# Gate and up matmuls of a feed-forward stage on 256 tokens at a time

## The reference, cut to what matters

```python
D_MODEL = 1024; SEQ = 512; D_FF = 2816
...
x = x + mix @ w_out[l]
h2 = rms_norm(x, g_ffn[l])
x = x + (jax.nn.silu(h2 @ w_ffn_gate[l]) * (h2 @ w_ffn_up[l])) @ w_ffn_down[l]
```

## Time and profile before

| | |
|---|---|
| median of 2 timed runs | 974.32 us (973.59 to 975.04) |
| span of the profiled execution, first to last instruction | 970.9 us |
| TensorE busy in the span | 915.0 us, 94%, 4492 matmuls |
| weight loads busy | 756.9 us, 78%, 4492 loads |
| VectorE, ScalarE busy | 398.1 us (41%), 361.3 us (37%) |
| stage of L1399 | 602.0 to 842.1 us of the span |

### The profile page before, as it was taken

How to read it: one execution, slowest core, us unless ns; L and a number is a source line. 1 busy time by engine, 2 the same in 40 slices (tenths; PEclk the granted TensorE clock), 3 DMA queues, 4 the chain that set the end, 5 groups by cost and what they waited for, 6 DMA issues and landing times.

```text
span 970.9 us, 13078 instructions
## 1 busy us (share of the span) xinstructions
PE 915.0 (94%) x4492; PEld 756.9 (78%) x4492; DVE 398.1 (41%) x554; ACT 361.3 (37%) x532; POOL 189.3 (19%) x256
## 2 busy tenths in 40 slices
PE   5189979999999899999999998999999999999998
PEld 4167868888888788888888787788888888788886
DVE  4036432657782333333347835332323232333334
ACT  5032223544424455554533324333334433332231
POOL 5069998820002010101142001000000000000000
PEclk9679989999999999999999999999999999999999
DMA  6239432493435444342262431323232323222312
GB/s 177 33 130 177 163 115 87 141 201 111 149 131 161 160 123 134 96 129 68 60 204 87 165 99 62 108 86 108 86 107 87 100 94 99 96 87 86 108 65 87
DMA packets 100382, 110.91 MB, mean 114 GB/s; under 512 B 25472, under 2 KB 66608, under 8 KB 100352
## 3 DMA queue, kind: packets, MB, share of 16 engines
q1 hardware_dynamic: 93440, 96.34, 32.5%
q0 software_dynamic: 3744, 7.89, 3.7%
q10 hardware_dynamic: 3168, 6.29, 1.7%
HBM read 94.42 MB, written 16.06 MB: 114 GB/s over the span
## 4 chain that ended last, share of the span: by engine, by line
PE 76%; POOL 9%; SPq 6%; DVE 4%; DMA 2%; ACT 1%; issue 1%; POOLq 0%; ACTq 0%; DVEq 0%
PE ps L1160 30%; PE ps L1399 24%; PE ps L1414 12%; POOL early L434 8%; SPq L298 4%; PE ps L1308 3%; PE ps L1282 2%; PE ps L1285 1%; PE ps L1294 1%; SPq L357 1%; DMA late<-in_x 1%; PE ps L1340 1%; DVE w_lo L600 1%; DMA late<-z_d 1%; PE ps L1235 1%
## 5 line engine op out<-in xcount | busy, mean ns | idle before, releaser
L600 DVE TENSOR_TENSOR w_lo<-w_raw,w_hi 128x1024 fp32r<-128x1024 f32 x142 | 191.9, 1351 | 363.3 <-ACT w_hi L594 362.1
L594 ACT ACTIVATE w_hi<-w_raw 128x1024 fp32r<-128x1024 f32 x142 | 150.5, 1060 | 401.5 <-PE ps L1160 162.4
L1399 PE MATMUL ps<-hT_hi,w_hi 128*128 128x512 f32 x352 | 137.1, 390 | 2.0 <-DVE hT_lo L822 1.6
L1160 PE MATMUL ps<-w_hi,hT_hi 128*128 128x512 f32 x352 | 137.6, 391 | 1.5 <-DVE w_lo L600 1.5
L1160 PE MATMUL ps<-w_lo,hT_hi 128*128 128x512 f32 x352 | 137.0, 389 | 0.0
L1160 PE MATMUL ps<-w_hi,hT_lo 128*128 128x512 f32 x352 | 137.0, 389 | 0.0
L1399 PE MATMUL ps<-hT_hi,w_lo 128*128 128x512 f32 x352 | 137.0, 389 | 0.0
L1399 PE MATMUL ps<-hT_lo,w_hi 128*128 128x512 f32 x352 | 136.9, 389 | 0.0
L434 POOL TENSOR_TENSOR early<-early 128x16 f32<-128x16 f32 (+7 forms) x137 | 114.3, 835 | 44.2 <-DVE gqk L853 33.5
L1160 PE MATMUL ps<-hT_hi,w_hi 128*128 128x512 f32 x160 | 69.2, 433 | 26.1 <-DVE w_lo L600 24.4
L1160 PEld LDWEIGHTS ps<-w_hi,hT_hi 128*128 128x128 f32 x352 | 66.1, 188 | 16.5 <-DVE w_lo L600 2.4
(11 more groups left out here) (188 smaller groups left out, 1124.0 us busy)
## 6 DMA issues: line engine op xcount, KB each, us to landing
w_raw<-in_w_in SPq DMA_DIRECT2D x112, 256.0 KB, 3.2
w_raw<-in_w_ffn_gate SPq DMA_DIRECT2D x44, 256.0 KB, 2.8
w_raw<-in_w_ffn_up SPq DMA_DIRECT2D x44, 256.0 KB, 3.0
w_raw<-in_w_ffn_down SPq DMA_DIRECT2D x44, 256.0 KB, 2.8
z_d<-early ACTq DMA_DIRECT2D x6, 1024.0 KB, 4.4
late<-z_d SPq DMA_DIRECT2D x96, 64.0 KB
w_raw<-in_w_out SPq DMA_DIRECT2D x16, 256.0 KB, 3.0
z_d<-early SPq DMA_DIRECT2D x3, 1024.0 KB, 4.2
```

What stands on the lines that cost most here:

```text
L594: nc.scalar.activation(w_hi[:, j % WSPL], w_raw[:, j % WRAW], ACT.Copy).then_inc(w_hi_done, 1)
L600: nc.vector.tensor_tensor(w_lo[:, j % WSPL], w_raw[:, j % WRAW], w_hi[:, j % WSPL].bitcast(F32), ALU.subtract).then_inc(w_lo_done, 1)
L1160: ins = T.matmul(ps[:, m], lhsT, rhs, start=first and h == 0 and k == 0, stop=last and h == 1 and k == 2)
L1399: ins = T.matmul(ps[:, m], (w_hi, w_lo)[b][:, j % WSPL, at_w:at_w + P], h_acts[a][:, 2 * j + h, :], start=j == 0 and h == 0 and k == 0, st ...
```

## The change

The loop over the two input blocks and the three products now stands inside a loop over two halves of the tokens. A matmul takes 256 columns of the activations and writes 256 columns of its bank. Within a bank and a tile, the first half of the tokens goes through all six weight blocks, and then the second half does. `start` and `stop` stand on the bank's very first and very last matmul, as before.

```diff
                         turned_rows(KT, j, m)
-                        for h in range(2):
-                            for k, (a, b) in enumerate(((0, 0), (1, 0), (0, 1))):
-                                at_w = m // 2 * 512 + h * 256 + m % 2 * P
-                                ins = T.matmul(ps[:, m], (w_hi, w_lo)[b][:, j % WSPL, at_w:at_w + P],
-                                               h_acts[a][:, 2 * j + h, :], start=j == 0 and h == 0 and k == 0,
-                                               stop=j == 3 and h == 1 and k == 2)
+                        for th in range(2):
+                            tok = slice(th * 256, (th + 1) * 256)
+                            for h in range(2):
+                                for k, (a, b) in enumerate(((0, 0), (1, 0), (0, 1))):
+                                    at_w = m // 2 * 512 + h * 256 + m % 2 * P
+                                    ins = T.matmul(ps[:, m, tok], (w_hi, w_lo)[b][:, j % WSPL, at_w:at_w + P],
+                                                   h_acts[a][:, 2 * j + h, tok],
+                                                   start=j == 0 and th == 0 and h == 0 and k == 0,
+                                                   stop=j == 3 and th == 1 and h == 1 and k == 2)
                         ins.then_inc(gemm_steps, 1)
```

## The result

The change makes the kernel slower: 986.89 us (985.76 to 988.02, 2 runs) against 974.32 (973.59 to 975.04), ratio 1.0147 with a 95% interval from 1.0096 to 1.0199 (the two medians alone give 1.0129, inside it). That is clear of no change, but within 2%. The forecast was 988.0.

The account below looks back on a forecast made before the run. TensorE was taken as the bound; 2112 half matmuls at 120.0 ns (253.4 us) against 1056 at 226.7 (239.4) add 14.0 us, less 0.3 credit, so 974.3 + 13.7 = 988.0 us, range 971 to 1001.

Parts of the forecast that it names:

- Bound: TensorE bounds the kernel; the L1399 matmuls hold 24% of the span, some 233 us, so their change goes into the total.
- Streaming, nothing: Gate and up matmuls: 2112 x 106.7 ns = 225.3 us of column streaming, the same as before.
- Weight loads, a floor of 112 ns: Doubled gate and up loads, 110 to 113 ns each, set a floor of about 112 ns per matmul, 236.5 us.
- The 13.3 ns, once per matmul: Time beside streaming in gate and up, paid per matmul: 120.0 ns per half matmul, 253.4 against 239.4 us, +14.0 us.
- two bounds: How the 13.3 ns scales for half matmuls: with the columns, 113.3 ns, or once per matmul or load, 120.0 ns.
- The credit of 0.3 us: First weight tile: 0.3 us of added matmul time falls into TensorE's wait for w_lo of the second tile.
- Hidden work, clock, instruction fetches: ScalarE and VectorE work stays covered, granted clock needn't fall, longer loop body costs nothing; no new wait.
- The 3.4 us around the span: Median of 974.32 us lies 3.4 us above the profiled span of 970.9, for what lies around the span.
- Rivals B: The extra in gate and up goes with the columns: 113.3 ns per half matmul, total 974.0 us; chance 0.16.
- B2: Gate and up extra: 3 ns fixed, 10.3 by columns; 114.9 ns per half matmul, total 977.3 us; chance 0.05.
- Rival C: Every gate and up pair pays load, then the 13.3 ns: 125.3 ns, +25.2 us, total 999.2 us; chance 0.24.
- D: Load not hidden behind a half matmul: 217 ns, +219, total 1193 us; chance 0.04 with other unforeseen losses.

Follow-up runs that it names:

- the thirds: Gate and up tokens cut in parts of 176, 176 and 160 columns instead of the change's two halves of 256; 1409.4 us.
- the bfloat16 pair: Kernel before with bfloat16 split operands in both feed-forward stages, 512 columns: 953.9 us, ratio 0.9801; the same plus the change, 256 columns: 955.1 us, ratio 0.9807.
- four pairs of the table: fp32r prices in ns at 512 and 256 columns: gate and up weights 128 wide 13.3, 13.3; 64 wide 16.7, 6.7; 32 wide 18.3, 11.1; down projection 19.1, 12.0.
- half-wide weights: Weight blocks loaded 64 outputs wide, half of gate and up outputs left out: twice 256 columns as in the change 969.2 us; 512 columns as before 973.1 us.
- The quarters: Gate and up tokens cut in four parts of 128 columns instead of the change's two halves of 256; 1635.1 us.

## Why the prediction was right

*Bound.* TensorE was the bound of the stage before and after, and ScalarE's wait grew by 13.2 us, about the stage's growth. Shown.

*Streaming, nothing.* The columns are the same, and 106.7 of the 120.0 ns are theirs. Consistent with all runs at the upper clock.

*Weight loads, a floor of 112 ns.* Shown in other kernels: within parts that were narrow enough to be load-bound at the upper clock (128, 176 and 192 columns), loads came 111 to 112 ns apart, 111.7 on average. The change stands 8 ns above that floor. Of the cover that was nearly gone I had said what a lack of it would cost, but not what comes below it: in the thirds the clock stayed down as well, and the span was 1408 us, in place of the 1087 that the load alone would give.

*The 13.3 ns, once per matmul.* The number was right to the tenth, 120.0, and it decided the forecast: 2112 x 120.0 = 253.4. The reason given for it holds in part, so the right number owes something to luck. Against a pure share of the columns, which would give 113.3, stands the 120.0. That it belongs to 4-byte operands is shown by the bfloat16 pair, where the price is 2.5 ns at both widths; whether to their stream or to their longer load is not. But "one price per matmul" is no rule. In the down projection the price fell from 19.1 to 12.0 when the columns were halved, and with narrower weights it moved between 6.7 and 18.3 without following the length of the load. At 256 columns it was lower than at 512 in three of the four pairs of the table. I took the right end from two bounds; in the down projection the same choice was 6 ns off (125.1 expected, 118.7 measured). And half-wide weights took 6.7 of the 13.3 ns off the very shape of the change, which a price per matmul alone wouldn't allow. One row was read one-sidedly: of the two 256-column matmuls in the earlier trace rows the "at most 3 ns" is the second's alone (216 ns). The first is followed by the second only after 320 ns, 107 above its streaming, in all 24 such pairs of the trace, and the prediction says nothing of it.

*The credit of 0.3 us.* Measured 0.28, the shrunken wait for the second tile.

*Hidden work, clock, instruction fetches.* No new wait, clock 1.00, the same 17 and 13 packets. The clock was right by a weak argument, and so by luck too: the stretch that I leaned on the earlier trace rows was plain fp32, and with 128 columns of fp32r, starts just as dense, the clock fell 1.8 us into the stage and stayed down. *The 3.4 us around the span* were taken wrongly and without effect on the sum: every timed run on record that has both numbers is 1.6 to 1.8 us above its own span, and the rest is the difference between two executions.

*Rivals B (113.3) and B2 (114.9)* are refuted by 120.0 for this stage, though 113.3 is what half-wide weights gave. *Rival C (125.3)* is refuted twice, by 120.0 and by the load-bound rows at 111.7, where its 13.3 would have to show. *D* is refuted by every load that starts with a matmul.

*Sum.* Forecast +13.7 us, stage measured +13.8, medians +12.6.

**Open.** What sets the price of an fp32r matmul. It is there at 2.4 GHz and gone at 1.2 (where the earlier trace rows show starts 0.43 us apart), it is down to 2.5 ns with 2-byte operands, and it comes in patterns of unequal distances as well as in a constant one. The prediction's idea, that load and stream get in each other's way, is argued and not shown; it doesn't say why narrower weights raise the price at 512 columns. No run here varied the addresses alone.

## What to carry to other kernels

In this kernel each matmul brings its own weight load, also when the weights repeat, so cutting the streamed side doubles the loads and any price per matmul. Compare the streamed time of one matmul with the load-bound distance in the same trace, here 112 ns for 128x128 in fp32r, before cutting. 256 columns stream for 107 ns, just below it, and cost 1.5%; parts of 176 and 160 cost 45% and 128 cost 68%, most of it through the clock. Look at the granted clock of the stage, and not at the distances alone. Where matmuls are the bound and operands are split anyway, look at the type of the splits: two bfloat16 parts in place of two fp32r parts took about 2% off, for less exact products.

## What the runs showed that I had not expected

The granted clock stayed at 1.2 GHz for 898 us of the stage (128 columns per matmul) and 675 us (176 and 160), with loads back to back without a pause. At that clock a load took 213 ns in place of 112, so the stage was slow twice over. In four of the fourteen traces the clock fell within 2 us of this stage's start, in one of them before a stage of 512-column matmuls. The quarters and the thirds got the full clock back only behind the stage, in the down projection with its 512 columns.

A narrower weight load can go with a slower matmul beside it: at 512 columns 226.7, 230.0 and 231.7 ns for weights 128, 64 and 32 wide.
